# A two-layer transformer kernel in full fp32 precision: w_down's product in both MLPs by Strassen's scheme, seven products of quarters instead of eight

## The chip, the cores and the metric

The kernel runs on one core of one Trainium2 chip. The metric is the device time of one execution in microseconds (us). Before the change it is 2845.04 us, the median of three runs (2844.16 to 2845.36). TensorE (PE) multiplies matrices, VectorE (DVE), ScalarE (ACT) and GpSimd (POOL) do elementwise work, SyncE (SP) issues the loads. SBUF is the on-chip memory; PSUM holds TensorE's results in eight banks of 512 fp32 columns.

## The reference, cut to what matters

Two transformer blocks on 1024 tokens of width 1024, in fp32. Each ends in an MLP of hidden width 4096:

```python
# block 1
h = _rmsnorm(x, g_mlp) * (1.0 + sc2) + sh2
u = jnp.square(jax.nn.relu(jnp.einsum('bsd,df->bsf', h, w_up)))
x = x + gt2 * jnp.einsum('bsf,fd->bsd', u, w_down)
# block 2
u = rms_norm(h, norm_mlp)
h = h + jnp.square(jax.nn.relu(u @ w_up)) @ w_down
```

In front of them stand a modulation, an indexed attention, a convolution, a pooling mixer and a gated delta rule; the change touches none of these. `gt2` is a row of 1024 gate values, the same for each token.

## The kernel before, in words

Precision. A matmul here takes fp32r operands, which hold fewer bits than fp32. Each fp32 operand is therefore split in a high part (a copy into an fp32r tile) and a low part (original minus high part), and each product of two tiles is three matmuls: high by high, high by low, low by high (lines 1975 to 1977 for `cm`, 1990 to 1992 for `tm`).

Order. There is no scheduler. Each engine has its own program, written out by hand, which runs in order; semaphores (`sem(...)`, `wait_ge`, `then_inc`) hold them together. The MLP is a function `mlp` in each of the five programs, called with k = 0 for block 1 and k = 1 for block 2.

The MLP. The hidden width is cut in 8 groups (`GROUPS`) of 512. The first group and the last are written out, the middle ones are a hardware loop (`Fori`). In a group:

- `up` (TensorE, `cm`): bank b = 4 * half + s of PSUM gets 128 hidden rows s by 512 tokens of `half`, over 8 slices of the width: 24 matmuls of 128x128 by 128x512. Eight of these make 192 matmuls. All eight banks are full afterwards.
- `unit` (ACT and DVE): relu into `act_r` (L1120), square on DVE (L1685), high part on ACT (L1124), low part on DVE (L1690), one bank at a time.
- `down` (TensorE, `tm`): for two halves th of the tokens, two halves j of the 1024 output columns and two slices kk of the hidden rows, four token tiles i: 6 matmuls each, again 192 in all. A bank is full after kk = 1.
- DVE then adds the bank to `x`, which lies in SBUF (L1698, k = 1). For k = 0 it first multiplies by the gate into `tmp2` (L1702), then adds (L1705).

Weights. SP loads 512 KB tiles into four places of `raw`; POOL makes `w_hi` (L730) and `w_lo` (L733) from them; there are four places of each, and eight weight tiles in a group (four for `up`, four for `down`). `split_done` counts the low parts and lets TensorE go and SP load again.

After the last group of MLP 0, `last0` on DVE interleaves the final sums with the norm of the next block (`times_g` L1333, `xn` L1346, `norm_lo2` L1353), and TensorE's `after_last0` puts transposes between the last parts of `down`.

## Time and profile before

| | |
|---|---|
| median of three runs | 2845.04 us |
| time of the profiled execution | 2844.08 us |
| its span | 2842.3 us |
| its mean granted TensorE clock | 0.97 |
| busy PE / DVE / ACT / POOL | 93% / 59% / 27% / 40% |
| HBM | 53 GB/s over the span |

The span is the time from the first to the last instruction in the trace. Idle time of an engine is what it spent waiting. A matmul's record is longer than its share of the engine, since matmuls are pipelined: the distance from one start to the next is what one costs.
### The profile page before, as it was taken

What the parts mean: (1) busy time and instruction counts of PE and PEld (TensorE: products, weight loads), DVE (VectorE), ACT (ScalarE), POOL (GpSimd) and SP (SyncE); (2) the same over time, 40 slices, a digit from 0 to 9 for tenths busy, and PEclk for the clock granted to TensorE, in tenths of its full rate; (3) what the DMA queues carried; (4) which work ended last, traced back from release to release, by engine and by line L of the source; (5) the groups of instructions that cost most, each with busy time, mean ns of one, the idle gap of its engine ahead of it and who ended that gap; (6) DMA issues with size and microseconds to landing.
All of it is one profiled execution on the core that took longest, in us unless ns stands there. A gap on an engine that the chain in (4) does not pass through costs nothing.

```text
span 2842.3 us, 37279 instructions
## 1 busy us (share of the span) xinstructions
PE 2649.1 (93%) x14704; PEld 2164.4 (76%) x14704; DVE 1686.9 (59%) x2230; ACT 774.5 (27%) x1426; POOL 1124.9 (40%) x774
## 2 busy tenths in 40 slices
PE   4999888999999999999999989788799999999998
PEld 4867766777878888888886768677588888888887
DVE  6268988763865665665765784577335423444335
ACT  4235366634230001110023442243223100011102
POOL 2431465443653443443532323332263534434432
PEclk8999999999999999999999999899799999999999
DMA  6201032001311111111212110000321111111111
GB/s 221 67 12 34 30 99 73 16 23 68 133 58 39 53 52 37 59 44 44 63 38 96 38 37 30 2 2 2 111 90 45 52 37 59 48 40 59 42 46 59
DMA packets 142499, 153.49 MB, mean 54 GB/s; under 512 B 7183, under 2 KB 105252, under 8 KB 142374
## 3 DMA queue, kind: packets, MB, share of 16 engines
q1 hardware_dynamic: 137088, 143.97, 15.9%
q10 hardware_dynamic: 5286, 7.79, 0.8%
q8 instruction: 86, 1.41, 0.2%
q14 instruction: 39, 0.32, 0.0%
HBM read 143.35 MB, written 8.39 MB: 53 GB/s over the span
## 4 chain that ended last, share of the span: by engine, by line
PE 78%; DVE 11%; ACT 5%; issue 4%; DMA 1%; POOL 0%; ACTq 0%; SPq 0%; DVEq 0%; POOLq 0%
PE ps L1990 12%; PE ps L1991 11%; PE ps L1992 11%; PE ps L1975 11%; PE ps L1977 11%; PE ps L1976 11%; ACT sel_out L991 2%; PE ps L2384 2%; DVE yt L1801 2%; PE ps L2066 2%; DVE yt L1790 1%; PE ps L2144 1%; PE ps L1958 1%; DVE score L1510 1%; PE ps L2133 1%
## 5 line engine op out<-in xcount | busy, mean ns | idle before, releaser
L1975 PE MATMUL ps<-h_hi,w_hi 128*128 128x512 f32 x1472 | 585.1, 398 | 10.1 <-issue 5.6
L1976 PE MATMUL ps<-h_lo,w_hi 128*128 128x512 f32 x1472 | 574.9, 391 | 0.0
L1977 PE MATMUL ps<-h_hi,w_lo 128*128 128x512 f32 x1472 | 574.7, 390 | 0.0
L730 POOL TENSOR_TENSOR w_hi<-raw,zero 128x1024 fp32r<-128x1024 f32 x128 | 243.7, 1904 | 781.1 <-PE ps L1977 398.2
L1990 PE MATMUL ps<-w_hi,u_hi 128*128 128x512 f32 x1024 | 399.2, 390 | 0.0
L1991 PE MATMUL ps<-w_lo,u_hi 128*128 128x512 f32 x1024 | 399.1, 390 | 0.0
L1992 PE MATMUL ps<-w_hi,u_lo 128*128 128x512 f32 x1024 | 399.0, 390 | 0.0
L1120 ACT ACTIVATE act_r<-ps 128x512 f32<-128x512 f32 x128 | 76.5, 598 | 1131.5 <-PE ps L1977 1131.5
L1685 DVE TENSOR_TENSOR act_r<-act_r 128x512 f32<-128x512 f32 x128 | 165.7, 1295 | 330.6 <-ACT act_r L1120 330.6
L733 POOL TENSOR_TENSOR w_lo<-raw,w_hi 128x1024 fp32r<-128x1024 f32 x128 | 338.1, 2642 | 10.1
L1975 PEld LDWEIGHTS ps<-h_hi,w_hi 128*128 128x128 f32 x1472 | 277.8, 189 | 77.6 <-issue 17.2
L1976 PEld LDWEIGHTS ps<-h_lo,w_hi 128*128 128x128 f32 x1472 | 277.9, 189 | 60.0 <-issue 3.7
L1977 PEld LDWEIGHTS ps<-h_hi,w_lo 128*128 128x128 f32 x1472 | 277.4, 188 | 58.5
L1690 DVE TENSOR_TENSOR u_lo<-act_r,u_hi 128x512 fp32r<-128x512 f32 x128 | 226.8, 1781 | 0.0
L1990 PEld LDWEIGHTS ps<-w_hi,u_hi 128*128 128x128 f32 x1024 | 192.8, 188 | 40.0
L1992 PEld LDWEIGHTS ps<-w_hi,u_lo 128*128 128x128 f32 x1024 | 192.6, 188 | 40.2
L1991 PEld LDWEIGHTS ps<-w_lo,u_hi 128*128 128x128 f32 x1024 | 192.6, 188 | 40.0
L1698 DVE TENSOR_TENSOR x<-x,ps 128x512 f32<-128x512 f32 x128 | 88.0, 688 | 212.2 <-PE ps L1992 212.2
L1990 PE MATMUL ps<-w_hi,h_hi 128*128 128x512 f32 (+2 forms) x512 | 185.1, 362 | 18.5 <-DVE h_lo L1916 7.3
L1991 PE MATMUL ps<-w_lo,h_hi 128*128 128x512 f32 (+2 forms) x512 | 183.2, 358 | 0.0
L1992 PE MATMUL ps<-w_hi,h_lo 128*128 128x512 f32 (+2 forms) x512 | 183.1, 358 | 0.0
L1705 DVE TENSOR_TENSOR x<-x,tmp 128x512 f32<-128x512 f32 x128 | 155.0, 1211 | 4.4
(426 smaller groups left out, 4062.4 us busy)
## 6 DMA issues: line engine op xcount, KB each, us to landing
raw<-in_w_up_dram SPq DMA_DIRECT2D x64, 512.0 KB, 4.0
...
```

Source lines behind the costliest of these rows:

```text
L730: g_.tensor_tensor(w_hi[:, r, :], raw[:, r, :], zero.to_broadcast([P, 1024]), ALU.add).then_inc(sem("w_hi_done"), 1)
L733: g_.tensor_tensor(w_lo[:, r, :], raw[:, r, :], w_hi[:, r, :].bitcast(F32), ALU.subtract).then_inc(sem("split_done"), 1)
L1685: v.tensor_tensor(act_r[:, b % 4, :], act_r[:, b % 4, :], act_r[:, b % 4, :], ALU.mult).then_inc(sem(f"u_sq{k}"), 1)
L1690: v.tensor_tensor(u_lo[c // 4][:, c % 4, :], act_r[:, c % 4, :], u_hi[c // 4][:, c % 4, :].bitcast(F32), ALU.subtract).then_inc(sem(f"u_lo ...
L1698: v.tensor_tensor(x[:, t, cols], x[:, t, cols], ps[:, n % 8, :], ALU.add).then_inc(sem(f"down_out{k}"), 1)
L1705: v.tensor_tensor(x[:, t, cols], x[:, t, cols], tmp2[:, n % 2, :], ALU.add).then_inc(sem(f"x_sum{k}"), 1)
L1975: mm(ps[:, bank, :], wh, h_hi[:, k, cols], start=(k == 0), stop=False)
L1976: mm(ps[:, bank, :], wh, h_lo[:, k, cols], start=False, stop=False)
L1977: last = mm(ps[:, bank, :], wl, h_hi[:, k, cols], start=False, stop=(k == NK - 1))
L1990: mm(o, hi[:, k0 + k, tok], wh, start=(start and k == 0), stop=False)
L1991: mm(o, hi[:, k0 + k, tok], wl, start=False, stop=False)
L1992: last = mm(o, lo[:, k0 + k, tok], wh, start=False, stop=(stop and k == 1))
```

## The change

The product of each group but the last is taken as a 2 x 2 product of quarters in the form with seven products (Winograd's variant of Strassen's scheme): `u` (1024 tokens by 512 hidden) is cut in A11, A12, A21, A22 of 512 tokens by 256 hidden, and `w_down`'s part (512 hidden by 1024 columns) in quarters of 256 by 512. Seven sums or differences of each side are multiplied; a product is four token tiles of 6 matmuls. Products 0, 2, 4 and 6 run on banks 4 to 7, products 1, 3 and 5 on banks 0 to 3. Product 2 adds to what product 0 left in the banks, and so on (`start` is set for products 0, 1 and 5 only), and after each product DVE adds the banks, as they then stand, to the quarter of `x` that this partial sum belongs to (`out`, 28 tile adds in a group instead of 16). The last group keeps eight products.

Around it:

- `u_f` holds all eight squared tiles in fp32. ACT's relu writes it, DVE squares as max(ps, 0) * u_f in one instruction (`squared`).
- DVE makes the four sums of u (`mix`, 128x1024 each) and seven low parts (`low`, 128x1024 each).
- ACT makes all high parts, those of the weights too (`w_high`, `u_high`, 128x1024 each): 11 and 7 in a group.
- POOL makes four differences of weights (`mix`) in `raw`, 11 low parts, and for k = 0 multiplies the gate into the four loaded tiles of `w_down` (`gated`). The tile add of k = 0 is then the same single instruction as that of k = 1.
- SP's loop over groups is unrolled, with the same eight 512 KB loads in a group.
- In the first group POOL makes `w_hi` of the four `up` tiles with `tensor_copy` instead of an add of zero.

The core of the diff:

```diff
@@ sizes @@
+        SG = GROUPS - 1
+        UPS, PRODUCTS = 4, 7
+        ITEMS = UPS + PRODUCTS
+        UP_SLOT = (3, 0, 1, 2)
+        DOWN_RAW = (3, 3, 3, 0, 1, 2, 3)
+        OUTS = 4 * PRODUCTS
+        SQ = 12
+        A21, A22, A11, A12 = (slice(2 * i, 2 * i + 2) for i in range(4))
...
@@ SP @@
+                for g in range(SG):
+                    for r, (j, kk) in enumerate(((1, 1), (1, 0), (0, 1), (0, 0))):
+                        sp.wait_ge(sem("split_done"), g * ITEMS + (m0 + r + 1))
+                        load_down(g, r, j, kk)
+                    for e in range(UPS):
+                        sp.wait_ge(sem("split_done"), g * ITEMS + (m0 + UPS + (5, 5, 7, 7)[e]))
+                        load_up(g + 1, e, UP_SLOT[e])
...
@@ POOL @@
+                def low(m, r, slot):
+                    pool.wait_ge(sem("w_hi_done"), m)
+                    g_.tensor_tensor(w_lo[:, slot, :], raw[:, r, :], w_hi[:, slot, :].bitcast(F32),
                                      ALU.subtract).then_inc(sem("split_done"), 1)
+                def gated(g, r, j):
+                    pool.wait_ge(raw_in[r], g * 32 + (raw0 + 32))
+                    w = v3(raw[:, r, :], 2)
+                    g_.tensor_tensor(w, w, gate2[:, j * HALF:(j + 1) * HALF].unsqueeze(1).to_broadcast([P, 2, HALF]),
+                                     ALU.mult).then_inc(sem("w_mixed"), 1)
+                def mix(dst, one, other):
+                    g_.tensor_tensor(raw[:, dst, :], raw[:, one, :], raw[:, other, :], ALU.subtract).then_inc(sem("w_mixed"), 1)
...
+                    def down_low(q):
+                        low(g * ITEMS + (m0 + UPS + q + 1), DOWN_RAW[q], q % 4)
...
+                    down_low(0)
+                    if k == 0:
+                        pool.wait_ge(sem("w_mixed"), g * mixes + (mix0 + 4))
+                    here(1)
+                    mix(3, 1, 3)
+                    down_low(1)
+                    here(0)
+                    mix(3, 0, 3)
+                    mix(1, 0, 1)
+                    down_low(2)
+                    here(2)
+                    mix(3, 2, 3)
+                    for q in range(3, PRODUCTS):
+                        down_low(q)
+                    for e in range(UPS):
+                        low(g * ITEMS + (m0 + ITEMS + e + 1), e, UP_SLOT[e])
...
+                    pool.wait_ge(sem(before[e][0]), before[e][1])
+                    pool.wait_ge(raw_in[e], raw0 + 16)
+                    g_.tensor_copy(w_hi[:, e, :], raw[:, e, :]).then_inc(sem("w_hi_done"), 1)
+                    low(m0 + e + 1, e, e)
...
@@ ACT @@
+                def relu(g, b):
+                    act.wait_ge(sem(f"up_full{k}"), g * 8 + (b + 1))
+                    s.activation(u_f[:, b, :], ps[:, b, :], ACT.Relu).then_inc(sem(f"up_relu{k}"), 1)
+
+                def w_high(slot, r):
+                    s.activation(w_hi[:, slot, :], raw[:, r, :], ACT.Copy).then_inc(sem("w_hi_done"), 1)
+
+                def u_high(dst, src, need):
+                    act.wait_ge(sem(f"u_sq{k}"), need)
+                    s.activation(dst, src, ACT.Copy).then_inc(sem(f"u_hi{k}"), 1)
+
+                def down_high(g, q):
+                    if q == 0 and k == 0:
+                        act.wait_ge(sem("w_mixed"), g * mixes + (mix0 + 4))
+                    if q in (0, 3, 5):
+                        act.wait_ge(raw_in[DOWN_RAW[q]], g * 32 + (raw0 + 32))
+                    else:
+                        act.wait_ge(sem("w_mixed"), g * mixes + (mix0 + mixes - 4 + {1: 1, 2: 2, 4: 3, 6: 4}[q]))
+                    w_high(q % 4, DOWN_RAW[q])
+
+                def group(g, after):
+                    for b in range(8):
+                        relu(g, b)
+                        after(b)
+                        if b >= 4:
+                            down_high(g, b - 4)
+                        if b == 4:
+                            u_high(us_hi[1], u_mix, g * SQ + 5)
+                        if b == 5:
+                            u_high(us_hi[0], u_f[:, A11, :], g * SQ + 7)
+                        if b == 6:
+                            u_high(us_hi[2], u_mix, g * SQ + 8)
...
+                    for p in range(3):
+                        act.wait_ge(sem(f"down_full{k}"), g * OUTS + 4 * (p + 1))
+                        down_high(g, 4 + p)
+                        if p == 0:
+                            u_high(us_hi[0], u_mix, g * SQ + 12)
+                        else:
+                            u_high(us_hi[p], u_f[:, A21 if p == 1 else A12, :], g * SQ + 11)
+                    for e in range(UPS):
+                        act.wait_ge(sem(f"down_full{k}"), g * OUTS + 4 * (4 + e))
+                        act.wait_ge(raw_in[e], g * 32 + (raw0 + 48))
+                        w_high(UP_SLOT[e], e)
+                        if e == 0:
+                            u_high(us_hi[0], u_f[:, A22, :], g * SQ + 11)
...
@@ DVE @@
+                def squared(g, b):
+                    dve.wait_ge(sem(f"up_relu{k}"), g * 8 + (b + 1))
+                    v.scalar_tensor_tensor(u_f[:, b, :], ps[:, b, :], 0.0, u_f[:, b, :], ALU.max,
+                                           ALU.mult).then_inc(sem(f"u_sq{k}"), 1)
+
+                def mix(dst, one, other, op, need):
+                    dve.wait_ge(sem(f"u_sq{k}"), need)
+                    v.tensor_tensor(dst, one, other, op).then_inc(sem(f"u_sq{k}"), 1)
+
+                def low(dst, src, high, need):
+                    dve.wait_ge(sem(f"u_hi{k}"), need)
+                    v.tensor_tensor(dst, src, high.bitcast(F32), ALU.subtract).then_inc(sem(f"u_lo{k}"), 1)
+
+                def out(g, p):
+                    row, j = ((1, 0), (0, 1), (1, 1), (1, 1), (0, 1), (1, 0), (0, 0))[p]
+                    for i in range(4):
+                        o = x[:, 4 * row + i, j * HALF:(j + 1) * HALF]
+                        dve.wait_ge(sem(f"down_full{k}"), g * OUTS + (4 * p + i + 1))
+                        if p == 3:
+                            dve.wait_ge(sem(f"down_out{k}"), g * OUTS + (4 * (p - 1) + i + 1))
+                        v.tensor_tensor(o, o, ps[:, 4 * ((p + 1) % 2) + i, :], ALU.add).then_inc(sem(f"down_out{k}"), 1)
+
+                def group(g, after):
+                    n = g * PRODUCTS
+                    for b in range(8):
+                        squared(g, b)
+                        after(b)
+                        if b == 3:
+                            mix(u_mix, u_f[:, A21, :], u_f[:, A22, :], ALU.add, g * SQ + 4)
+                        if b == 4:
+                            low(us_lo[1], u_mix, us_hi[1], n + 1)
+                        if b == 5:
+                            mix(u_mix, u_mix, u_f[:, A11, :], ALU.subtract, g * SQ + 7)
+                            mix(u_f[:, A21, :], u_f[:, A11, :], u_f[:, A21, :], ALU.subtract, g * SQ + 7)
+                            low(us_lo[0], u_f[:, A11, :], us_hi[0], n + 2)
+                        if b == 6:
+                            low(us_lo[2], u_mix, us_hi[2], n + 3)
+                    mix(u_mix, u_f[:, A12, :], u_mix, ALU.subtract, g * SQ + 11)
+                    out(g, 0)
+                    low(us_lo[0], u_mix, us_hi[0], n + 4)
+                    out(g, 1)
+                    low(us_lo[1], u_f[:, A21, :], us_hi[1], n + 5)
+                    out(g, 2)
+                    low(us_lo[2], u_f[:, A12, :], us_hi[2], n + 6)
+                    out(g, 3)
+                    low(us_lo[0], u_f[:, A22, :], us_hi[0], n + 7)
+                    for p in range(4, PRODUCTS):
+                        out(g, p)
...
+                def down(n):
                     j, t = n // 4 % 2, 4 * (n // 8) + n % 4
                     cols = slice(j * HALF, (j + 1) * HALF)
-                    dve.wait_ge(sem(f"down_full{k}"), g * 16 + (n + 1))
-                    if gate is None:
-                        v.tensor_tensor(x[:, t, cols], x[:, t, cols], ps[:, n % 8, :],
-                                        ALU.add).then_inc(sem(f"down_out{k}"), 1)
-                    else:
-                        dve.wait_ge(sem(f"x_sum{k}"), g * 16 + (n + 1))
-                        v.tensor_tensor(tmp2[:, n % 2, :], ps[:, n % 8, :], gate[:, cols],
-                                        ALU.mult).then_inc(sem(f"down_out{k}"), 1)
-                        dve.wait_ge(sem(f"down_out{k}"), g * 16 + (n + 1))
-                        v.tensor_tensor(x[:, t, cols], x[:, t, cols], tmp2[:, n % 2, :],
-                                        ALU.add).then_inc(sem(f"x_sum{k}"), 1)
-
-                dve.sem_inc(sem(f"u_lo{k}"), 4)
-                if gate is not None:
-                    dve.sem_inc(sem(f"x_sum{k}"), 2)
-                for b in range(9):
-                    unit(0, b)
+                    dve.wait_ge(sem(f"down_full{k}"), OUT_LAST + n + 1)
+                    v.tensor_tensor(x[:, t, cols], x[:, t, cols], ps[:, n % 8, :],
+                                    ALU.add).then_inc(sem(f"down_out{k}"), 1)
...
@@ PE @@
+                def chained(slot, i, hi, lo, fresh, b):
+                    tok = slice(i * P, (i + 1) * P)
+                    for c in range(2):
+                        wh, wl = (v3(w[:, slot, :], 2)[:, c, :] for w in (w_hi, w_lo))
+                        for n, (l, r) in enumerate(((hi, wh), (hi, wl), (lo, wh))):
+                            last = mm(ps[:, b, :], l[:, c, tok], r, start=(fresh and c == 0 and n == 0),
+                                      stop=(c == 1 and n == 2), skip_group_check=True)
+                    return last
+
+                def product(g, p):
+                    pe.wait_ge(sem("split_done"), g * ITEMS + (m0 + UPS + p + 1))
+                    pe.wait_ge(sem(f"u_lo{k}"), g * PRODUCTS + max(2, p + 1))
+                    for i in range(4):
+                        b = 4 * ((p + 1) % 2) + i
+                        if p < 2:
+                            pe.wait_ge(sem(f"u_sq{k}"), g * SQ + (1, 2, 3, 4, 6, 7, 10, 11)[b])
+                        else:
+                            pe.wait_ge(sem(f"down_out{k}"), g * OUTS + (4 * (p - 2) + i + 1))
+                        last = chained(p % 4, i, us_hi[p % 3], us_lo[p % 3], p in (0, 1, 5), b)
+                        last.then_inc(sem(f"down_full{k}"), 1)
...
```

The order on DVE, in the first group of MLP 0, from the fifth bank on. Before, each bank's square is followed by the low part of the bank ahead of it, and then come the pairs of gate and add:

```order
L1685 TENSOR_TENSOR act_r<-act_r 128x512 [waits up_relu0]
L1690 TENSOR_TENSOR u_lo_60<-act_r,u_hi_58 128x512 [waits u_hi0]
L1685 TENSOR_TENSOR act_r<-act_r 128x512 [waits up_relu0]
L1690 TENSOR_TENSOR u_lo_60<-act_r,u_hi_58 128x512 [waits u_hi0] x2
L1702 TENSOR_TENSOR tmp_151<-ps,gate_170 128x512 [waits x_sum0,down_full0]
L1705 TENSOR_TENSOR x<-x,tmp_151 128x512 [waits down_out0]
```

And now, the same place on DVE (`us_lo_152` to `us_lo_154` are us_lo[0] to us_lo[2], `us_hi_149` to `us_hi_151` us_hi[0] to us_hi[2]):

```order
L1793 SCALAR_TENSOR_TENSOR u_f<-ps,u_f 128x512 [waits up_relu0]
L1802 TENSOR_TENSOR us_lo_153<-u_mix,us_hi_150 128x1024 [waits u_hi0]
L1793 SCALAR_TENSOR_TENSOR u_f<-ps,u_f 128x512 [waits up_relu0]
L1798 TENSOR_TENSOR u_mix<-u_mix,u_f 128x1024 [waits u_sq0]
L1798 TENSOR_TENSOR u_f<-u_f 128x1024 [waits u_sq0]
L1802 TENSOR_TENSOR us_lo_152<-u_f,us_hi_149 128x1024 [waits u_hi0]
L1793 SCALAR_TENSOR_TENSOR u_f<-ps,u_f 128x512 [waits up_relu0]
L1802 TENSOR_TENSOR us_lo_154<-u_mix,us_hi_151 128x1024 [waits u_hi0]
L1793 SCALAR_TENSOR_TENSOR u_f<-ps,u_f 128x512 [waits up_relu0]
L1798 TENSOR_TENSOR u_mix<-u_f,u_mix 128x1024 [waits u_sq0]
L1811 TENSOR_TENSOR x<-x,ps 128x512 [waits down_full0] x4
```

Sums and low parts of twice the width now stand between the squares of banks 4 to 7, and the square of bank 7 (the last L1793) comes behind the low part for product 2.

The order on ACT at the same banks. Before, it is relu and high part in turn:

```order
L1120 ACTIVATE act_r<-ps 128x512 [waits u_lo0,up_full0]
L1124 ACTIVATE u_hi_58<-act_r 128x512 [waits u_sq0]
L1120 ACTIVATE act_r<-ps 128x512 [waits u_lo0,up_full0]
L1124 ACTIVATE u_hi_58<-act_r 128x512 [waits u_sq0]
L1120 ACTIVATE act_r<-ps 128x512 [waits u_lo0,up_full0]
```

And now, from the relu of bank 5 to that of bank 7:

```order
L1178 ACTIVATE u_f<-ps 128x512 [waits up_full0]
L1181 ACTIVATE w_hi<-raw 128x1024 [waits w_mixed]
L1185 ACTIVATE us_hi_149<-u_f 128x1024 [waits u_sq0]
L1178 ACTIVATE u_f<-ps 128x512 [waits up_full0]
L1181 ACTIVATE w_hi<-raw 128x1024 [waits w_mixed]
L1185 ACTIVATE us_hi_151<-u_mix 128x1024 [waits u_sq0]
L1178 ACTIVATE u_f<-ps 128x512 [waits up_full0]
```

Two high parts of weights, each of which waits for a difference that POOL makes (`w_mixed`), now stand ahead of the high part of u and of the relu of the next bank.

## Rows read from the trace of the kernel before

**Rows 1.** The page: busy time by engine, and the granted clock in 40 slices.

```profile
PE 2649.1 (93%) x14704; PEld 2164.4 (76%) x14704; DVE 1686.9 (59%) x2230; ACT 774.5 (27%) x1426; POOL 1124.9 (40%) x774
...
PEclk8999999999999999999999999899799999999999
```

**Rows 2.** The page's chain of what ended last, by engine.

```profile
PE 78%; DVE 11%; ACT 5%; issue 4%; DMA 1%; POOL 0%; ACTq 0%; SPq 0%; DVEq 0%; POOLq 0%
```

**Rows 3.** Windows: busy us of each engine (instructions), granted clock, DMA share, GB/s.

```profile
820.00:1480.00 660.00, 660.00 (x2913) 546.49 (x2913) 415.75 (x368) 75.78 (x134) 277.47 (x122) 1.00 0.16 48
1480.00:1520.00 40.00, 35.10 (x157) 28.26 (x156) 33.41 (x41) 19.76 (x38) 16.11 (x8) 0.91 0.23 79
2160.00:2820.00 660.00, 660.00 (x2914) 546.49 (x2913) 270.99 (x244) 73.97 (x132) 267.99 (x120) 1.00 0.14 45
```

**Rows 4.** ACT's timeline in MLP 0, loop: start, us, instruction, idle before and releaser.

```profile
893.91 0.60 ACT L1120 ACTIVATE act_r<-ps 128x512 f32<-128x512 f32 x1 [45.81 <-PE ps L1977]
...
904.79 0.60 ACT L1120 ACTIVATE act_r<-ps 128x512 f32<-128x512 f32 x1 [4.32 <-PE ps L1977]
910.23 0.60 ACT L1120 ACTIVATE act_r<-ps 128x512 f32<-128x512 f32 x1 [4.32 <-PE ps L1977]
...
980.95 0.60 ACT L1120 ACTIVATE act_r<-ps 128x512 f32<-128x512 f32 x1 [45.81 <-PE ps L1977]
```

**Rows 5.** The page's costliest groups: count | busy us, mean ns | idle before.

```profile
L1990 PE MATMUL ps<-w_hi,u_hi 128*128 128x512 f32 x1024 | 399.2, 390 | 0.0
```

**Rows 6.** PE's timeline in an up product of MLP 0.

```profile
895.30 0.39 PE L1976 MATMUL ps<-h_lo,w_hi 128*128 128x512 f32 x1
895.53 0.39 PE L1977 MATMUL ps<-h_hi,w_lo 128*128 128x512 f32 x1
```

**Rows 7.** By line: duration ns min/median/max, first and last start, forms.

```profile
L1698 DVE TENSOR_TENSOR x<-x,ps x128: 679/687/689, 2188.0 to 2835.6; 128x512 f32<-128x512 f32 x128
L1685 DVE TENSOR_TENSOR act_r<-act_r x128: 682/1830/1939, 803.9 to 2791.1; 128x512 f32<-128x512 f32 x128
L733 POOL TENSOR_TENSOR w_lo<-raw,w_hi x128: 2385/2724/2934, 792.3 to 2792.5; 128x1024 fp32r<-128x1024 f32 x128
L773 POOL TENSOR_TENSOR w_lo<-raw,w_hi x36: 2347/2392/3390, 1483.0 to 2110.0; 128x1024 fp32r<-128x1024 f32 x36
L1333 DVE TENSOR_TENSOR x<-x,frow x8: 1207/1221/1227, 1477.3 to 1517.0; 128x1024 f32<-128x1024 f32 x8
L868 ACT ACTIVATE junk<-x x48: 1040/1060/1075, 15.9 to 2836.3; 128x1024 f32<-128x1024 f32 x48
```

**Rows 8.** Timelines of POOL and DVE beside each other in MLP 0.

```profile
917.77 2.72 POOL L733 TENSOR_TENSOR w_lo<-raw,w_hi 128x1024 fp32r<-128x1024 f32 x1
...
918.16 2.88 DVE L1690 TENSOR_TENSOR u_lo<-act_r,u_hi 128x512 fp32r<-128x512 f32 x1
```

**Rows 9.** Start of MLP 0: POOL's timeline, a later copy on it, then PE's.

```profile
790.36 1.89 POOL L730 TENSOR_TENSOR w_hi<-raw,zero 128x1024 fp32r<-128x1024 f32 x1 [21.43 <-PE ps L1992]
...
1542.98 1.04 POOL L771 CAST w_hi<-raw 128x1024 fp32r<-128x1024 f32 x1 [31.82 <-PE ps L1977]
...
795.11 0.76 PE L1975 MATMUL ps<-h_hi,w_hi 128*128 128x512 f32 x1 [4.83 <-issue]
...
796.52 0.63 PE L1975 MATMUL ps<-h_hi,w_hi 128*128 128x512 f32 x1
796.95 0.63 PE L1976 MATMUL ps<-h_lo,w_hi 128*128 128x512 f32 x1
```

**Rows 10.** End of MLP 0: DVE's timeline, then PE's transposes.

```profile
1476.72 0.69 DVE L1705 TENSOR_TENSOR x<-x,tmp 128x512 f32<-128x512 f32 x1
...
1498.12 0.69 DVE L1702 TENSOR_TENSOR tmp<-ps,gate 128x512 f32<-128x512 f32 x1
...
1493.34 0.66 PE L1958 MATMUL ps<-ident,xn 128*128 128x128 f32 x4 [1.06 <-DVE tmp L1702]
...
1498.86 1.12 PE L1958 MATMUL ps<-ident,xn 128*128 128x128 f32 x4 [0.22 <-DVE tmp L1702]
```

242 lines of the change are left out of this document (122 added, 120 removed).

## The prediction, written before the change was run

> **What bounds the kernel now.** I read the page's busy row first: TensorE is busy for 93% of the span, and its granted clock is at 9 or 8 tenths in all but a few slices [rows 1]. Busy matmul time can mislead, since records overlap, so I went on to the chain of what ended last: 78% of it is TensorE [rows 2]. Then to the stages. In 820 to 1480 us (MLP 0) and 2160 to 2820 us (MLP 1) TensorE has no idle time at all and the full clock, while DVE is busy for 416 and 271 of 660 us and POOL for 277 and 268 [rows 3]. So in both MLPs nothing but TensorE sets the pace, and a matmul taken away there is worth its spacing.
>
> That spacing: two matmuls start 0.227 us apart, though each record is 0.39 us long [rows 6]. ACT's relus agree: one every 5.44 us, which is 24 matmuls at 0.2267, and the first relu of a group comes 87.04 us after that of the group before [rows 4], which is 384 x 0.2267. The page counts 1024 high-by-high matmuls of `down` for the two MLPs [rows 5], so 64 x 3 = 192 in each of 16 groups: half of a group is `down`.
>
> **Term 1, the products.** Seven products instead of eight leave 168 of these 192: 24 matmuls or 5.44 us less in a group, in 7 groups of each of 2 MLPs: 14 x 5.44 = 76.2 us. The matmuls kept have the same shape, 128x128 by 128x512, and the same three operand pairs, so I keep their spacing. A group becomes 360 x 0.2267 = 81.6 us.
>
> Here the Trainium skill says otherwise: its page "TensorE: Matmul & The Clock Gate", section "Back-to-back issue gap", gives a sustained spacing of about 131 ns for 512 columns. By that figure the 336 matmuls would be worth only 44 us, an estimate from that page; the trace has 226.7 ns for these fp32r operands, and the trace decides.
>
> **Term 2, whether the other engines keep up.** By sums they do. DVE per group: 8 squares and 28 tile adds of 0.69 (one operand in PSUM; L1698 stays at 0.679 to 0.689 in all 128 cases, beside POOL's work too [rows 7]) are 24.8 us; 4 sums and 7 low parts of 128x1024, like L1333's 1.22 [rows 7], are 13.4; together 38, of 81.6. But instructions with both operands in SBUF wait for POOL: L1685 has 0.68 at least and 1.83 in the median [rows 7], and a low part that DVE started at 918.16 ended at 921.04, 0.55 after the POOL instruction that ended at 920.49 [rows 8]. So each of the 11 wide ones may wait for one POOL instruction: with 2.4 each, 38 + 26 = 64 us, still under 81.6. POOL: 11 low parts, 4 differences and for k = 0 four gate products, 19 in all. None of the last two kinds is in the trace; the nearest rows are two-operand ones of the same size, 2.35 at least (L773) and 3.39 at most (L773 beside DVE) [rows 7]. I take 2.4 alone and 3.3 beside DVE: at most 63 us. ACT: 8 relus of 0.60 [rows 4] and 18 copies of 128x1024 at 1.06, like L868 [rows 7]: 24 us. Loads are the same 4 MB a group.
>
> What could break is the order in time around the start of product 0. I count from the end of up product 4, so that products 5, 6, 7 end at 5.44, 10.88, 16.32 and product 0 starts at 16.32; its fourth tile, which needs bank 7 squared, starts at 16.32 + 3 x 1.36 = 20.4. The chain, with a relu 0.2 after its bank is full: relu 4 and the high part of weight 0 end at 1.8 on ACT. POOL's low part 0 ends at 4.2. DVE's low part for product 1 waits for it, ends at 5.3, and holds up POOL's first difference, which ends at 7.6. ACT has waited for it: high part of weight 1 at 8.7, that of A11 at 9.7. DVE's two sums end at 8.7 and 9.8; POOL's low part 1 (issued 8.75, held up by the second) at 12.1, and DVE's low part of A11 at 13.2, 3.1 us ahead of product 0. POOL's second difference ends at 15.5. Only then can ACT go on: weight 2 at 16.5, the high part for product 2 at 17.5, and relu 7 behind them at 18.0, 1.1 us later than its bank allows. DVE's low part for product 2 waits for POOL's third difference and ends at 19.0, and the square of bank 7 behind it at 19.7. TensorE wants it at 20.4, so there is 0.7 us to spare. Letting POOL in ahead of DVE's second sum moves the end to about 20.0. After that point slack grows: product 2 needs bank 4 drained at 27.2, DVE drains it at about 23; product 3's operands are ready some 3 us ahead, later ones 3 to 10. The next group's `up` weights are split 5 us before use.
>
> So term 2 is 0 in my sum. It can't be below 0, since TensorE has no idle time left in these windows. Upward its bound is open, and priced under the rivals.
>
> **Term 3, the start of MLP 0.** TensorE stands still for 4.83 us until the first weights are split. POOL starts with `w_hi` at 790.36, 1.89 us long; the copy that takes its place is 1.04 us at 1542.98 [rows 9]. This lies on the path: 0.85 us gained, 0 if the copy is held up. MLP 1 starts without such a gap.
>
> **Term 4, the end of MLP 0.** The window 1480 to 1520 has 35.1 of 40 us busy and a clock of 0.91 [rows 3]: TensorE's transposes for the next norm wait for DVE's `tmp`, which frees the banks; they go at 1493.34 and the last at 1498.86 [rows 10]. Between lie four pairs of gate and add, the adds up to 2 us long beside POOL. After the change each pair is one add of 0.69. The last bank before is free at 1498.12 + 0.69 = 1498.8; the first came free at 1493.3. With 0.65 steps the last is free at about 1495.2, and the first pass (`x` complete, 1476.72 + 0.69) moves up by 0.7: about 1494.5. That gains 4.3 us, and a little of the half clock that follows; I take 4.5, between 0 (if something else is late there, such as `xn`) and 7 (all of the idle 4.9 and the clock). In later work nothing overtakes it: TensorE is at once busy with `w_in_2`.
>
> **The sum.** Against the profiled execution's own 2844.08 us (span 2842.3 and 1.8 around it): 76.2 + 0.85 + 4.5 = 81.5, so 2762.5. The median of the runs is 0.96 above that execution: 2763.5 us, 2.9% less.
>
> **Rivals.**
> 1. TensorE waits at product 0 in every group. The chain above has five POOL instructions in a row and 0.7 us to spare; if the in-place differences take 2.9 instead of 2.4, or semaphores add 0.2 per link, bank 7 is 0.5 to 3 us late. For it: ACT, DVE and POOL wait for each other there in turn. Against: each duration above is already the contended one. At 1.5 us it is 14 x 1.5 = 21 us: 2784.
> 2. The waits ahead of each tile cost something by themselves. Now 28 tiles of a group wait for a bank, 16 did before. If each drained the pipeline it would cost 0.39 - 0.227 = 0.163 us [rows 6], 14 x 28 x 0.163 = 64 us: 2827. Against: the waits before cost nothing at all [rows 3].
> 3. Short gaps lower the clock. After the 4.83 us without work, matmuls start 0.43 us apart (796.52, 796.95 [rows 9]), the 1.2 GHz level. Were each stall at product 0 followed by a dozen of these, 12 x 0.2 x 14 = 34 us come on top: about 2797 without the stalls. Against: gaps of 0.6 to 1 us are not in these windows, so the trace cannot tell. The Trainium skill's page "TensorE: Matmul & The Clock Gate", section "A second HAM failure mode: psum-queue depth-cycling", describes this for frequent micro-idles between groups of matmuls; no run here shows it yet.
> 4. Slower than before. The same chain, but so late that it eats the gain: it must be 5.8 us (81.5 / 14) beyond the 0.7 spare, which over five POOL links is 1.3 us each, so a POOL instruction beside DVE of 4.6 us instead of 3.3. At 5.0 each group would lose 5 x 1.7 - 0.7 = 7.8: 2763.5 + 109 = 2873. Against: none of 164 such rows is above 3.39 [rows 7]; it needs DVE to get in ahead of POOL twice each time.
>
> **How the numbers follow.** Forecast 0.66; rival 1 0.22; rival 2 0.05; rival 3 0.03; rival 4 0.04. The bounds of terms 3 and 4 give the forecast 2761 to 2769. Below I add 2 us for what the three runs spread: 2759. Above I go into rival 1 as far as a stall of 1.9 us a group: 2790. That holds about 8 in 10. A measurement of this kernel can tell about 0.2% (5.7 us) from no change. Faster: all but rival 4, and a sliver where it just cancels: 0.95; same 0.01; slower 0.04.
>
> **What would show it.** Right: relus of bank 0 81.6 us apart in the loop, no idle time on TensorE there, `x<-x,ps` at 0.69, the fourth tile of product 0 not waiting. Rival 1: TensorE idle before a product 0 tile with the release by DVE's L1793, groups of 82 to 85 us. Rival 2: tiles of more than 1.36 us. Rival 3: clock under 1.00 in the windows. It would be wrong as a whole if groups stayed above 86 us, or if the spacing of the product matmuls differed from 0.227.

## The result, and the profile after

The changed kernel takes 2768.76 us (median of four runs, 2763.87 to 2769.25) against 2844.6 us before (median of four, 2842.42 to 2845.36): a ratio of 0.9731, 95% interval 0.9714 to 0.9748. The forecast was 2763.5 us, the range 2759 to 2790. The profiled execution took 2768.58 us with a span of 2766.8; that is 75.5 us less than before's in both numbers.

The changed kernel's page, the rows that answer to [rows 1] and [rows 5], and DVE's tile adds (columns of the groups: count | busy us, mean ns | idle us before, releaser):

```profile
PE 2582.5 (93%) x14368; PEld 2106.0 (76%) x14368; DVE 1701.5 (61%) x2304; ACT 972.8 (35%) x1566; POOL 1247.7 (45%) x784
...
PEclk8999999999999999999999999899699999999999
...
L2389 PE MATMUL ps<-w_hi,us_hi 128*128 128x512 f32 x784 | 306.8, 391 | 0.0
L1811 DVE TENSOR_TENSOR x<-x,ps 128x512 f32<-128x512 f32 x392 | 248.5, 678 | 66.1 <-PE ps L2389 66.1
```

TensorE has 14368 matmuls instead of 14704: exactly the 14 x 24 = 336 that the change drops. DVE, ACT and POOL have more work in total, and the share of TensorE has not moved. Windows of the changed kernel, for [rows 3]: the loops of both MLPs, and the end of MLP 0.

```profile
820.00:1400.00 580.00, 580.00 (x2548) 478.13 (x2547) 339.05 (x338) 164.07 (x189) 356.99 (x133) 1.00 0.17 51
1455.00:1495.00 40.00, 38.69 (x194) 28.99 (x192) 24.59 (x35) 16.68 (x31) 9.59 (x6) 1.00 0.45 151
2090.00:2740.00 650.00, 650.00 (x2871) 536.04 (x2870) 365.23 (x365) 192.08 (x232) 304.93 (x112) 1.00 0.15 47
```

TensorE is still busy without a break in both loops, at the full clock. The 40 us at the end of MLP 0 have 38.69 busy and a clock of 1.00, where [rows 3] had 35.10 and 0.91. Now the groups, by ACT's timeline (start, us, instruction; the relu of bank 0 of two groups in the loop):

```profile
890.16 0.60 ACT L1178 ACTIVATE u_f<-ps 128x512 f32<-128x512 f32 x1 [4.38 <-PE ps L2117]
...
972.16 0.60 ACT L1178 ACTIVATE u_f<-ps 128x512 f32<-128x512 f32 x1 [4.38 <-PE ps L2117]
```

A group takes 82.00 us. It was 87.04 [rows 4], and the prediction said 81.60. The 0.40 us between stand in TensorE's timeline: the first matmuls of products 1, 2, 3 and 4.

```profile
933.48 0.39 PE L2389 MATMUL ps<-w_hi,us_hi 128*128 128x512 f32 x1
...
938.92 0.39 PE L2389 MATMUL ps<-w_hi,us_hi 128*128 128x512 f32 x1
...
944.53 0.39 PE L2389 MATMUL ps<-w_hi,us_hi 128*128 128x512 f32 x1
...
950.00 0.39 PE L2389 MATMUL ps<-w_hi,us_hi 128*128 128x512 f32 x1
```

Product 1 lasts 5.44 us, as predicted. Product 2 lasts 5.61: its 24 matmuls start 233.8 ns apart instead of 226.7, with no idle time between them, and the next few are still a little late (5.47). Product 5 does the same. That is 2 x (0.17 + 0.03) = 0.40 us. These two read the third of three stationary tiles, `us_hi[2]` and `us_lo[2]` (the tile of product p is p % 3).

**The chain before product 0.** The prediction worked out a chain of links over ACT, POOL and DVE and left 0.7 us to spare at its end. The same stretch of the changed kernel, counted from 911.72, where up product 4 ends (0.2 us before the relu), POOL first, then DVE, then ACT:

```profile
913.54 2.39 POOL L757 TENSOR_TENSOR w_lo<-raw,w_hi 128x1024 fp32r<-128x1024 f32 x1 [15.81 <-ACT w_hi L1181]
915.90 3.38 POOL L767 TENSOR_TENSOR raw<-raw 128x1024 f32<-128x1024 f32 x1
920.45 3.31 POOL L757 TENSOR_TENSOR w_lo<-raw,w_hi 128x1024 fp32r<-128x1024 f32 x1 [1.17 <-ACT w_hi L1181]
923.70 5.75 POOL L767 TENSOR_TENSOR raw<-raw 128x1024 f32<-128x1024 f32 x2
...
914.44 2.58 DVE L1802 TENSOR_TENSOR us_lo<-u_mix,us_hi 128x1024 fp32r<-128x1024 f32 x1 [1.20 <-ACT us_hi L1185]
...
929.16 1.37 DVE L1802 TENSOR_TENSOR us_lo<-u_mix,us_hi 128x1024 fp32r<-128x1024 f32 x1 [3.73 <-ACT us_hi L1185]
930.46 0.68 DVE L1793 SCALAR_TENSOR_TENSOR u_f<-ps,u_f 128x512 f32<-128x512 f32 x1
...
927.12 1.06 ACT L1181 ACTIVATE w_hi<-raw 128x1024 fp32r<-128x1024 f32 x1 [3.72 <-POOL raw L767]
```

| link | predicted end | measured end |
|---|---|---|
| POOL's low part 0 | 4.2 | 4.21 |
| POOL's first difference | 7.6 | 7.56 |
| POOL's low part 1 | 12.1 | 12.04 |
| ACT's high part of weight 2 | 16.5 | 16.46 |
| DVE's low part for product 2 | 19.0 | 18.81 |
| DVE's square of bank 7 | 19.7 | 19.42 |
| TensorE wants it | 20.4 | 20.40 |

So 0.98 us are left, and the fourth tile of product 0 does not wait. The low part at 914.44 shows the lock that the sum went by: 2.58 us for what takes DVE 1.2 alone, because it waits until POOL's low part is done at 915.93, and the POOL difference behind it takes 3.38 instead of 2.4. The Trainium skill's page "SBUF — State Buffer", section "Terms", says of the ports that DVE and GpSimd share that they are held for a whole instruction and that the loser is blocked fully; the trace agrees.

### The profile page after: what moved, and what is told of

It is laid out like the page before. It is cut to its first block, busy times and chain, and to the rows that moved or that the text cites. A ratio compares the mean times of both kernels' runs of the same rounds, so it can differ in the third digit from the quotient of the medians.

```text
span 2766.8 us, 36836 instructions
## 1 busy us (share of the span) xinstructions
PE 2582.5 (93%) x14368; PEld 2106.0 (76%) x14368; DVE 1701.5 (61%) x2304; ACT 972.8 (35%) x1566; POOL 1247.7 (45%) x784
## 4 chain that ended last, share of the span: by engine, by line
PE 78%; DVE 12%; ACT 5%; issue 4%; DMA 1%; POOL 0%; ACTq 0%; SPq 0%; DVEq 0%; POOLq 0%
PE ps L2389 19%; PE ps L2115 11%; PE ps L2117 11%; PE ps L2116 11%; PE ps L2130 4%; PE ps L2131 4%; PE ps L2132 4%; ACT sel_out L1048 2%; PE ps L2547 2%; PE ps L2206 2%; DVE yt L1941 2%; DVE yt L1930 1%; PE ps L2284 1%; PE ps L2098 1%; PE ps L2273 1%
## 5 line engine op out<-in xcount | busy, mean ns | idle before, releaser
L1181 ACT ACTIVATE w_hi<-raw 128x1024 fp32r<-128x1024 f32 x162 | 171.7, 1060 | 435.0 <-PE ps L2389 363.9
L1793 DVE SCALAR_TENSOR_TENSOR u_f<-ps,u_f 128x512 f32<-128x512 f32 x128 | 88.1, 688 | 371.6 <-ACT u_f L1178 371.6
L2389 PE MATMUL ps<-w_lo,us_hi 128*128 128x512 f32 x784 | 306.9, 391 | 0.0
L2389 PE MATMUL ps<-w_hi,us_hi 128*128 128x512 f32 x784 | 306.8, 391 | 0.0
L2389 PE MATMUL ps<-w_hi,us_lo 128*128 128x512 f32 x784 | 306.6, 391 | 0.0
L1811 DVE TENSOR_TENSOR x<-x,ps 128x512 f32<-128x512 f32 x392 | 248.5, 678 | 66.1 <-PE ps L2389 66.1
L1802 DVE TENSOR_TENSOR us_lo<-u_f,us_hi 128x1024 fp32r<-128x1024 f32 x62 | 169.4, 2731 | 12.6 <-ACT us_hi L1185 12.6
L767 POOL TENSOR_TENSOR raw<-raw 128x1024 f32<-128x1024 f32 x56 | 175.4, 3142 | 0.0
L2389 PEld LDWEIGHTS ps<-w_hi,us_hi 128*128 128x128 f32 x784 | 147.3, 188 | 32.5
L2389 PEld LDWEIGHTS ps<-w_hi,us_lo 128*128 128x128 f32 x784 | 147.3, 188 | 32.3
L2389 PEld LDWEIGHTS ps<-w_lo,us_hi 128*128 128x128 f32 x784 | 147.3, 188 | 32.1
```

The costliest lines, as they stand in the source:

```text
L767: g_.tensor_tensor(raw[:, dst, :], raw[:, one, :], raw[:, other, :], ALU.subtract).then_inc(sem("w_mixed"), 1)
L1181: s.activation(w_hi[:, slot, :], raw[:, r, :], ACT.Copy).then_inc(sem("w_hi_done"), 1)
L1802: v.tensor_tensor(dst, src, high.bitcast(F32), ALU.subtract).then_inc(sem(f"u_lo{k}"), 1)
L1811: v.tensor_tensor(o, o, ps[:, 4 * ((p + 1) % 2) + i, :], ALU.add).then_inc(sem(f"down_out{k}"), 1)
L2389: last = mm(ps[:, b, :], l[:, c, tok], r, start=(fresh and c == 0 and n == 0), stop=(c == 1 and n == 2), skip_group_check=True)
```

## The experiments

### Is the slow spacing a matter of alignment?

Theory A of the first four runs: `us[2]` starts 32 bytes past a multiple of 64 within a partition (AD = 202720), every other matmul operand at a multiple of 64, and a stationary operand placed so costs 7 to 8 ns a matmul. Rival B: the spacing comes from what the other engines do during products 2 and 5. Their edits:

```diff
e1_us2
-        U_AT = (AU + 16 * K1, AU + 24 * K1, AD + 4 * K1)
+        U_AT = (AU + 16 * K1, AU + 24 * K1, AD + 4 * K1 - 32)
e2_ad64   (AD and all behind it 32 bytes lower)
-        eps2 = small("eps2", [P, 1])
+        eps2 = at("eps2", [P, 1], F32, BASE - 32)
e8_base32   (all tiles 32 bytes lower)
-        BASE = 16512
+        BASE = 16480
e3_swap   (us[0] and us[2] change places; the last group follows)
-        U_AT = (AU + 16 * K1, AU + 24 * K1, AD + 4 * K1)
+        U_AT = (AD + 4 * K1, AU + 24 * K1, AU + 16 * K1)
```

> The changed kernel with one tile pair, us[2] (high and low part), 32 bytes lower in SBUF, so that it starts at a multiple of 64 bytes and no longer 32 bytes past one. Products 2 and 5 read it. Theory A (the place in SBUF of TensorE's stationary operand costs some 8 ns a matmul): both products at 226.7 ns a matmul instead of 233.8 to 235, the group at 81.60 to 81.65 us instead of 82.00, the kernel 14 x 0.4 = 5.6 us faster, about 2763. Rival B (these two products are slowed by what DVE, ACT and POOL do beside them): nothing changes, groups at 82.00, about 2769.

> The changed kernel with the whole last region of SBUF 32 bytes lower (one 4-byte constant moves below the first tile), so that us[2], ub_lo and all other tiles in it start at multiples of 64. Theory A: as for the one pair, and the two last groups lose their slow parts as well (some 0.6 us each): 2761 to 2763, the fastest so far. Rival B: about 2769.

> The changed kernel with the addresses of us[0] and us[2] exchanged: us[0] (products 0, 3 and 6) now starts 32 bytes past a multiple of 64. Theory A: products 0, 3, 6 slow (about 234 ns), 2 and 5 at 226.7, the group at 82.2 us, the kernel some 2.8 us slower than the changed one: about 2771. Rival B: products 2 and 5 stay the slow ones, 82.00.

> The changed kernel with every tile 32 bytes lower, so that x, the weights, h, u and us[0], us[1] start 32 bytes past a multiple of 64, and only the last region, with us[2], starts at one. Theory A, stationary operand alone: up products and products 0, 1, 3, 4, 6 at about 234 ns, 2 and 5 at 226.7, the group at 81.6 + 312 x 0.0075 = 83.9 us; over the whole kernel some 100 us more, 2840 to 2880. If the moving operand counts too, 2 and 5 are slow as well. Rival B: groups at 82.00 and about 2769.

| kernel | median us (runs) | ratio to before, 95% interval | a group in its trace |
|---|---|---|---|
| e1_us2 | 2761.12 (5) | 0.9716 [0.9700, 0.9732] | 81.97 |
| e2_ad64 | 2763.75 (5) | 0.9728 [0.9712, 0.9745] | 81.97 |
| e3_swap | 2764.98 (4) | 0.9734 [0.9714, 0.9754] | 82.20 |
| e8_base32 | 2766.3 (4) | 0.9737 [0.9720, 0.9755] | 82.00 |

By the medians alone e1_us2, 7.6 us under the changed kernel, would seem to bear theory A out. Its ratio's interval overlaps the changed kernel's, though (0.9714 to 0.9748), and its trace says no: a group takes 81.97, not 81.60. Aligning the tile takes 0.03 of the 0.40 us away. And in e8_base32 every operand that was at a multiple of 64 no longer is, the tile in AD is at one now, and the group is as long as before. Theory A fell. e3_swap then says what it is; its first matmuls of products 0, 1, 2, 3:

```profile
922.60 0.39 PE L2389 MATMUL ps<-w_hi,us_hi 128*128 128x512 f32 x1
...
928.22 0.39 PE L2389 MATMUL ps<-w_hi,us_hi 128*128 128x512 f32 x1
...
933.68 0.39 PE L2389 MATMUL ps<-w_hi,us_hi 128*128 128x512 f32 x1
...
939.12 0.39 PE L2389 MATMUL ps<-w_hi,us_hi 128*128 128x512 f32 x1
```

Now product 0 takes 5.62 us and product 2, slow in the changed kernel, 5.44; products 3 and 6 are slow like 0. These are the three that read `us[0]`, which lies in the region AD now, and three slow products instead of two make a group 0.20 longer. The slow spacing goes with the place. Rival B is out with it: the neighbours of the products are the same.

### Which place, and how much of it

Theory C: the region AD. It begins at byte 202720 of a partition, with the tile at 206816 to 215008; all other operands of the MLPs' matmuls end at 196736 or below (that a bound lies between is all that these runs show). e9_low gives the tile the place of `u_f`'s upper banks, and these banks go into AD, where only ACT and DVE touch them. e10_lohigh moves `us_hi[2]` alone. e12_best goes on from e9_low and writes the last group's `ub_lo`, also in AD until then, over the quarter that it is made from.

```diff
e9_low
-        u_f = at("u_f", [P, 8, HALF], F32, AU)
-        U_AT = (AU + 16 * K1, AU + 24 * K1, AD + 4 * K1)
+        U_AT = (AU + 16 * K1, AU + 24 * K1, AU + 8 * K1)
+        u_f = Pieces(at("u_fa", [P, 4, HALF], F32, AU), at("u_fb", [P, 4, HALF], F32, AD + 4 * K1))
e10_lohigh
+        us_hi[2] = at("us_hi2", [P, 2, HALF], F32R, AU + 12 * K1)
+        u_f = Pieces(at("u_fa", [P, 6, HALF], F32, AU), at("u_fb", [P, 2, HALF], F32, AD + 4 * K1))
e12_best, besides e9_low
-        ub_lo = at("ub_lo", [P, 2, HALF], F32R, AD + 16 * K1)
+        ub_lo = at("ub_lo", [P, 2, HALF], F32R, AU + 4 * K1)
```

> The changed kernel, with the third stationary tile (us_hi[2], us_lo[2]) at 8 to 16 KB of the region AU, where u_f's last four banks were, and these four banks where the tile was (4 to 12 KB of the region AD). Theory C (the slow spacing of 233.8 ns belongs to operands that lie in the region AD, not to the third tile as such, nor to products 2 and 5): all seven products at 226.7 ns, groups of 81.60 instead of 82.00 us, the last group's two parts with us[2] at 226.7 as well; 14 x 0.40 + 2 x 0.35 = 6.3 us less than the changed kernel, about 2762.5 by its profiled execution. Rival D (it belongs to two weight sets that are read 8 KB from what DVE or ScalarE write just then): u_f's banks lie beside the tile now, so 82.00 or more.

> The changed kernel with us_hi[2] moved to the last 4 KB of u_f's place (12 KB into the region AU) and us_lo[2] left in the region AD; u_f's last two banks take the freed 4 KB in AD. Of three matmuls of a product two now have a stationary operand outside AD, one inside. Theory C1 (each weight load from AD costs its 7.1 ns by itself): products 2 and 5 at 226.7 + 7.1 / 3 = 229.0 ns, groups of 81.71 us. Theory C2 (one operand there slows nearly all three, as in the last group, where ub_hi lies in AU and ub_lo in AD and its two parts went at 232.5 and 232.9): 232.7 ns, groups of 81.89.

> The version with us[2] in AU (groups of 81.60) and besides ub_lo written over the quarter it is made from, also in AU, so that no stationary operand of the two MLPs lies in AD. Theory C: the last group's two ub parts fall from 232.5 and 232.9 to 226.7 ns, 24 x 0.006 x 2 = 0.3 us an MLP, 0.6 in all; from the last group's first relu to the end 0.3 us shorter, which a median can't tell. Against the changed kernel in the same call: 6.3 + 0.6 = 6.9 us less, a ratio of 0.9975. Rival G (what the traces show inside the loops is given back in the middle part): no difference.

The last group's parts for the first half of the tokens read `us[2]` and `ub` in turn; in the changed kernel they went at 233.8, 232.5, 234.2 and 232.9 ns, which by 24 each over 226.7 is 0.64 us.

e9_low: 2758.38 us (four runs), ratio to before 0.9708 [0.9686, 0.973]. Its relu of bank 0 in two groups:

```profile
887.77 0.60 ACT L1189 ACTIVATE u_fa<-ps 128x512 f32<-128x512 f32 x1 [4.38 <-PE ps L2128]
...
969.37 0.60 ACT L1189 ACTIVATE u_fa<-ps 128x512 f32<-128x512 f32 x1 [4.38 <-PE ps L2128]
```

That is 81.60 us, the prediction's figure, in each of the 12 distances between groups in the two loops, and all seven products last 5.44. Theory C holds. D is out: the tile now lies next to `u_f`'s lower banks, which ACT and DVE write, and by D the group would have stayed at 82.00 or more. e10_lohigh has the same two rows 81.94 us apart:

```profile
886.09 0.60 ACT L1190 ACTIVATE u_fa<-ps 128x512 f32<-128x512 f32 x1 [4.38 <-PE ps L2129]
...
968.03 0.60 ACT L1190 ACTIVATE u_fa<-ps 128x512 f32<-128x512 f32 x1 [4.38 <-PE ps L2129]
```

0.34 of the 0.40 us remain though only one load of three comes from AD. C1 expected 81.71 and C2 81.89, so C2 is the nearer. Why one such operand slows its neighbours too stays open. In e12_best the last group's four first parts all go at 226.7 ns, and from its first relu to the end it takes 89.89 us, as in the kernel before, against 90.26 in e9_low and 90.58 in the changed kernel. It took 2757.1 us (four runs, 2753.36 to 2759.08), ratio to before 0.9707 [0.9684, 0.973]: the lowest median of the versions run, though 1.3 us under e9_low's is less than the runs can tell apart. The changed kernel again, beside it:

> The changed kernel again, for a comparison on the same chip as the others of this call: groups of 82.00 us, products 2 and 5 at 233.8 ns; its time as before within the runs' spread, 2764 to 2769 us.

It took 2764.06 us (four runs, 2755.36 to 2769.78), ratio to before 0.9743 [0.9717, 0.9768]; groups of 82.00 again. The ratio of the two medians is 0.9975, as expected, but the intervals overlap, so the 6.9 us rest on the traces. Much of the spread lies outside the change. The stretch between the MLPs goes at a granted clock of 0.92 in one execution and 0.95 in another, of the same kernel (first row: the changed kernel's first profiled execution, second: e14_after's):

```profile
1500.00:2060.00 560.00, 488.00 (x4080) 395.19 (x4079) 331.50 (x482) 178.80 (x318) 183.31 (x172) 0.92 0.11 37
```

```profile
1500.00:2060.00 560.00, 486.67 (x4114) 395.24 (x4113) 332.94 (x486) 177.65 (x317) 189.22 (x175) 0.95 0.12 39
```

From the first relu of MLP 0's last group to MLP 1's first relu it is 716.50 us in the first and 708.87 in the second, and MLP 0 starts 7.0 us earlier in the second. For e1_us2 this means: its trace has 716.56 us there, and of the 3.7 us by which its span is the shorter, 3.4 lie ahead of the first relu of MLP 0. Where its other four executions won time no trace shows; alignment is worth 14 x 0.03 = 0.4 us.

### Term 1: what a product costs

```diff
e11_eight
-                        last = chained(p % 4, i, us_hi[p % 3], us_lo[p % 3], p in (0, 1, 5), b)
+                        for twice in range(1 + (p == 5)):
+                            last = chained(p % 4, i, us_hi[p % 3], us_lo[p % 3], p in (0, 1, 5), b)
```

> The changed kernel with each tile of product 5 done twice into the same bank, the second pass starting anew, so that the result is the same and a group has 24 matmuls more. Term 1 of the prediction (the loop is bound by TensorE's matmul count alone, everything else has room): product 5 reads us[2], so 24 x 0.2338 = 5.61 us more in each of 14 groups, 87.61 us a group, 78.5 in all: 2847 us, no faster than the kernel before. Rival F (part of the 5 us a group came from something else that the change brought, as the chain's order or its fewer waits at DVE): groups well above or below 87.6.

```profile
893.91 0.60 ACT L1178 ACTIVATE u_f<-ps 128x512 f32<-128x512 f32 x1 [4.38 <-PE ps L2117]
...
981.52 0.60 ACT L1178 ACTIVATE u_f<-ps 128x512 f32<-128x512 f32 x1 [4.38 <-PE ps L2117]
```

A group takes 87.61 us, to the digit. In time it is 2838.45 us (ten runs, beside 2842.04 for the kernel before), ratio to before 1.0001 [0.9983, 1.0018]: with its eighth product back the kernel has no gain left that can be told from the noise. All that the loops gain is 24 matmuls a group.

### Term 2: how much room the chain has

```diff
e7_slack
+        w_pad = at("w_pad", [P, 1024], F32, AD)
...
+                    g_.tensor_tensor(w_pad, raw[:, 1, :], raw[:, 1, :], ALU.subtract)
                     mix(3, 1, 3)
```

> The changed kernel with one more POOL instruction in each group, a 128x1024 subtraction whose result nobody reads, ahead of the first difference of w_down's rows. It takes 2.4 us alone and up to 3.4 beside DVE. The chain of the prediction (five POOL instructions in a row, and bank 7's square about 1 us before product 0's fourth tile needs it): TensorE idles 1.4 to 2.4 us before that tile in each group, groups of 83.4 to 84.4 us, 14 x that: 2788 to 2803 us. Rival 1 in its stronger form (each link waits for DVE's turn too): over 3.5 us a group, above 2818. Rival E (bank 7 hangs on TensorE's own up product and POOL's chain has more room than the prediction worked out): no change, 2769.

It took 2777.21 us (four runs), ratio to before 0.9785 [0.9759, 0.9812] against the changed kernel's 0.9731. A group is 83.22 to 83.27 us in all but the first, 1.25 more; the expectation had 1.4 to 2.4 more and so was a little too high. POOL, DVE and TensorE (third and fourth tile of product 0) of e7_slack, then its window of the loop:

```profile
912.17 2.88 POOL L784 TENSOR_TENSOR w_pad<-raw 128x1024 f32<-128x1024 f32 x1
...
919.64 2.41 POOL L758 TENSOR_TENSOR w_lo<-raw,w_hi 128x1024 fp32r<-128x1024 f32 x1 [1.17 <-ACT w_hi L1183]
...
928.75 0.68 DVE L1795 SCALAR_TENSOR_TENSOR u_f<-ps,u_f 128x512 f32<-128x512 f32 x1
...
928.17 0.39 PE L2391 MATMUL ps<-w_hi,us_lo 128*128 128x512 f32 x1
929.49 0.50 PE L2391 MATMUL ps<-w_hi,us_hi 128*128 128x512 f32 x1 [0.93 <-DVE u_f L1795]
929.82 0.40 PE L2391 MATMUL ps<-w_lo,us_hi 128*128 128x512 f32 x1
```

```profile
820.00:1400.00 580.00, 573.48 (x2510) 470.39 (x2509) 337.75 (x330) 159.35 (x183) 371.35 (x140) 1.00 0.17 51
```

TensorE waits where the prediction's rival 1 put it, for the square of bank 7. The added instruction took 2.88 us, but POOL's low part 1 now runs without DVE beside it, 2.41 instead of 3.31, so the square comes only 2.0 us later. Less the 0.98 to spare, that is a stall of 1.0 to 1.1 us, and the pipeline starts again a little slower (0.33 to the next matmul): 1.25. The chain was real, and so was its margin. (14 x 1.25 = 17.5 us on the changed kernel's 2768.58 would be 2786; this execution took 2775.91, as the front part and the stretch between the MLPs were 5 us shorter each, and the added instruction does not touch them.) The window's clock stays at 1.00 with a stall of this size in each group. The Trainium skill's page "TensorE: Matmul & The Clock Gate", section "A second HAM failure mode: psum-queue depth-cycling", ties a falling clock to frequent micro-idles between groups of matmuls; here one of 0.93 us in each group of 83 us did not lower the clock, and the prediction's rival 3 gets no support.

### Terms 3 and 4: start and end of MLP 0

Each was tried alone on the kernel before. e6_copy only copies in the first group; e5_nogate leaves out MLP 0's product of each sum by the gate and so has one DVE instruction for a tile.

```diff
e6_copy   (first group only)
-                    g_.tensor_tensor(w_hi[:, r, :], raw[:, r, :], zero.to_broadcast([P, 1024]), ALU.add)
+                    g_.tensor_copy(w_hi[:, r, :], raw[:, r, :])
e5_nogate
-            mlp(0, 1, gate2, last0)
+            mlp(0, 1, None, last0)
```

> The kernel before, with only the first group's four w_hi made by a copy on POOL instead of an addition of zero. The prediction's term 3: TensorE's gap of 4.83 us at the start of MLP 0 becomes 3.98, and the first relu comes 12.1 us after POOL's first w_hi instead of 12.94. If the later three copies count too (three more w_hi, each 1.3 us shorter, while TensorE waits for each product's weights at half clock): 11.0 us as in the changed kernel, so that the whole of its 1.94 us is this edit's.

> The kernel before, with MLP 0's product of each sum by the gate left out, so that each tile at its end takes one DVE instruction from PSUM into x instead of two. From the last group's first relu to the transposes of the later norm (after the 128x8 products) it is 115.50 us before and 109.48 after the change. The prediction's term 4 (these pairs hold the banks, 4.5 us): 111.0. If the whole shortening at the end of MLP 0 hangs on them: 109.0 (6.66 us less: the 6.02 of the two traces and 0.64 of slower spacing in the changed kernel's last group). If it hangs on something else of the change (the order of the last group's parts): 115.

e6_copy (one run, 2841.13 us): POOL, TensorE's first matmul and the one from which the full clock is back, ACT's first relu.

```profile
790.76 1.04 POOL L731 CAST w_hi<-raw 128x1024 fp32r<-128x1024 f32 x1 [21.41 <-PE ps L1995]
...
794.65 0.76 PE L1978 MATMUL ps<-h_hi,w_hi 128*128 128x512 f32 x1 [3.96 <-issue]
...
797.35 0.46 PE L1978 MATMUL ps<-h_hi,w_hi 128*128 128x512 f32 x1
...
801.72 0.60 ACT L1123 ACTIVATE act_r<-ps 128x512 f32<-128x512 f32 x1 [7.86 <-PE ps L1980]
```

The gap shrinks from 4.83 [rows 9] to 3.96 us, as in term 3. But the relu comes 10.96 us after POOL's start, not 12.1 and not 12.94 as before: 0.86 us are gained up to TensorE's first matmul and 1.12 behind it. The expectation had named 11.0 for the case that the three later copies count too, but they can't be the reason: all this lies in the first up product, which reads one weight tile. After the gap of 4.83 us twelve matmuls started 0.43 us apart, the 1.2 GHz level of [rows 9]; here it is six. The changed kernel, the same place, has six as well, and 11.00 us from POOL's start to the relu:

```profile
793.59 1.04 POOL L799 CAST w_hi<-raw 128x1024 fp32r<-128x1024 f32 x1 [21.41 <-PE ps L2132]
...
797.47 0.77 PE L2115 MATMUL ps<-h_hi,w_hi 128*128 128x512 f32 x1 [3.95 <-issue]
...
800.17 0.52 PE L2115 MATMUL ps<-h_hi,w_hi 128*128 128x512 f32 x1
```

That the shorter gap brings fewer slow matmuls with it would be the wrong reading, though. e14_after is the same kernel as the changed one and has the same gap:

```profile
790.45 0.76 PE L2115 MATMUL ps<-h_hi,w_hi 128*128 128x512 f32 x1 [3.95 <-issue]
...
796.13 0.58 PE L2116 MATMUL ps<-h_lo,w_hi 128*128 128x512 f32 x1
796.55 0.40 PE L2117 MATMUL ps<-h_hi,w_lo 128*128 128x512 f32 x1
```

Here fourteen matmuls went at half clock, more than the twelve after the longer gap, and the relu came 12.48 us after POOL's start. Of the twelve traces with a gap of 3.95 or 3.96 us, nine have six or seven slow matmuls (10.95 to 11.21 us to the relu) and three, e14_after, e3_swap and e11_eight, have fourteen (12.46 to 12.49); the two with 4.83 us, before and e5_nogate, have twelve (12.94 and 12.95). So the copy is shown to give the 0.87 us of the gap. The 1.07 us behind it in the changed kernel's trace differ from execution to execution and are not shown to be owed to it.

e5_nogate (one run, 2837.0 us): TensorE's transposes, and the window of [rows 3].

```profile
1492.82 2.46 PE L1958 MATMUL ps<-ident,xn 128*128 128x128 f32 x16 [0.75 <-DVE x L1698]
```

```profile
1480.00:1520.00 40.00, 38.95 (x186) 31.40 (x185) 29.42 (x38) 18.67 (x36) 15.25 (x8) 1.00 0.40 137
```

All 16 transposes go in one piece with one wait of 0.75 us, where [rows 10] had four pieces and waits of 1.06, 0.79, 2.10 and 0.22. From the last group's first relu to the transposes after the 128x8 products it is 108.84 us against 115.50: 6.66 us less, the whole of what the change gained there. (The changed kernel has 109.48, with 0.64 for its operands in AD; e12_best, without these, has 108.83.) The transposes end 4.50 us sooner, the size of term 4: 3.42 of it is less waiting, and most of the rest is that two of the four pieces had gone at half clock (1.1 us instead of 0.66). The other 2.16 lie behind them: nine matmuls at half clock, which are gone, and a later wait of 0.74 us, which is 0.30 now. This second part varies too. e6_copy, which is the kernel before at this place, has the same four waits within 0.01 us but six slow matmuls, and 114.89 us; against it e5_nogate gains 6.05. The pairs of gate and add are the cause; the changed kernel's row is the same but for the line:

```profile
1459.68 2.45 PE L2098 MATMUL ps<-ident,xn 128*128 128x128 f32 x16 [0.76 <-DVE x L1844]
```

## Why the prediction came out right, and where it was off

| stretch | predicted, us | measured, us |
|---|---|---|
| term 1, 14 products | -76.2 | -70.6 (14 x 5.04) |
| term 2, stalls | 0 | 0 |
| term 3, start of MLP 0 | -0.85 | -1.94 (-0.87 the gap; the rest varies, as above) |
| term 4, end of MLP 0 | -4.5 | -6.66 |
| last group of each MLP (AD, as above; the second from its first relu to the end) | 0 | +0.64 and +0.69 |
| before MLP 0, code unchanged | 0 | +3.23 |
| between the MLPs, code unchanged | 0 | -0.89 |
| sum | -81.5 | -75.5 |

- Bound: right. Both loops had no idle time on TensorE before and have none now; e11_eight gives the whole gain back with one product.
- Term 1: right in its mechanism, off in one size. "The matmuls kept have the same shape (...), so I keep their spacing" is the sentence that failed: 48 of the 168 product matmuls read a tile in AD. The price is 0.40 us a group, 5.6 in all; e9_low takes it away and gets the predicted 81.60. The prediction did name a spacing other than 0.227 as what would show it wrong. No stationary operand of the MLPs lay in AD before, so their rows could not give it. But one place in the trace before could have raised the question: the 128x8 products, whose stationary tiles `ab_hi` and `ab_lo` lie at bytes 200832 to 201344 of a partition, just above 196736, with 512 columns and the full clock as in the MLPs. First and last of 24 matmuls of the kernel before:

```profile
1526.11 0.39 PE L2303 MATMUL ps<-h_hi,ab_hi 128*8 128x512 f32 x1
...
1531.42 0.39 PE L2305 MATMUL ps<-h_hi,ab_lo 128*8 128x512 f32 x1
```

  They start 230.9 ns apart, not 226.7. Whether their place does it or their 8 columns, no run tells.
- Term 2: right link by link, within 0.3 us at the end of the chain. Rival 1 had 0.22; the trace has it 0.98 us away, and in e7_slack one POOL instruction of 2.88 us brought it about. Rivals 2 (waits ahead of each tile) and 4 are not in the trace: tiles of product 1 take 1.36 us, waits and all, and POOL's low parts and differences take 3.41 at most. The prediction set its measured 226.7 ns against a sustained figure of the Trainium skill, 131 ns ("TensorE: Matmul & The Clock Gate", "Back-to-back issue gap"): the measured one decided rightly, and the product rows read here show none below 226.7.
- Terms 3 and 4: right up to the end of the wait (0.85 against 0.87) and of the transposes (4.5 against 4.50), and too small in what follows. Both gave little or nothing for the matmuls at half clock behind a wait. In the profiled executions what follows was 1.07 us shorter at the start and 2.16 at the end; as shown above, the first is not shown to come from the change, and the second varies by 0.6 us between executions. The upper bound of term 4, 7 us, had this in it ("all of the idle 4.9 and the clock").
- The rest: the front part was 3.23 us longer in this execution. It is unchanged code; in e14_after, the same kernel, POOL's first copy of MLP 0 comes at 786.57 instead of 793.59. Of the 6.0 us by which the profiled execution missed the sum, the place in AD is 6.9 (5.6 and the last groups' 1.33), the two ends give 3.3 back, and 2.3 lie in code that the change does not touch. That errors of both signs left the total only 6 us off is partly luck; what was right by its working is the bound, the count of matmuls, the chain, and what held TensorE up at the two ends.
